# Sharing the weight splits of units 28 to 63 between VectorE and GpSimd in a two-block kernel

## The reference

```python
# first block
h = _rmsnorm(x, norm_g); proj = h @ w_in + b_in                  # 1024 -> 8192
u, v, za, ab, ab_gate, zb, g_a, g_b = split(proj)
y_a = spatial_gating(gelu(u), gelu(v), za)                        # layer norm, 8 masked 128x128 mixes
y_b = conformer_conv(ab * sigmoid(ab_gate), zb)                   # 31-tap depthwise conv, group norm, silu
merged = sigmoid(g_a) * (y_a @ w_pa) + sigmoid(g_b) * (y_b @ w_pb)
x = x + merged @ w_out
x = x + sigmoid(_rmsnorm(x, ple_norm_g) @ w_ple_gate) * (p @ w_ple)
x = _rmsnorm(x, final_g)
# second block
proj = rms_norm(x) @ w_in_2      # qa ka va qb kb vb qi ki wi xc yc gates
y_a = causal attention with a bias table (8 heads)
y_b = attention over the 64 keys with the largest index scores (8 heads)
y_c = rg_lru(conv4(xc)) * gelu(yc)
merged = g0 * (y_a @ w_pa) + g1 * (y_b @ w_pb) + g2 * (y_c @ w_pc)
x = x + merged @ w_o
x = x + relu(rms_norm(x) @ w_up) ** 2 @ w_down
return rms_norm(x)
```

## Time and profile before

| | us |
|---|---|
| median of 3 runs | 820.05 |
| lowest and highest | 819.63, 822.71 |
| the profiled execution | 820.05 |
| its span | 818.2 |

### The profile page before, as it was taken

How to read it: one execution, slowest core, us unless ns; L and a number is a source line. 1 busy time by engine, 2 the same in 40 slices (tenths; PEclk the granted TensorE clock), 3 DMA queues, 4 the chain that set the end, 5 groups by cost and what they waited for, 6 DMA issues and landing times.

```text
span 818.2 us, 14164 instructions
## 1 busy us (share of the span) xinstructions
PE 794.9 (97%) x5914; PEld 751.3 (92%) x5914; DVE 539.8 (66%) x870; ACT 393.7 (48%) x472; POOL 163.4 (20%) x101
## 2 busy tenths in 40 slices
PE   5999999999999998999999999999999999999996
PEld 4998999999989998899999989898999999999995
DVE  4674693999766757766898665555677554545553
ACT  4634354555653457623564435445335644444342
POOL 2898587972000010000003210000000000000000
PEclk8999999999999999989999999999999999999999
DMA  8765454546526586454446544534544655565521
GB/s 251 235 205 157 141 161 140 173 148 209 178 90 205 180 299 191 114 171 155 155 126 196 171 148 133 155 130 146 190 155 155 214 170 183 203 205 189 165 107 52
DMA packets 120625, 138.15 MB, mean 169 GB/s; under 512 B 6704, under 2 KB 111480, under 8 KB 120569
## 3 DMA queue, kind: packets, MB, share of 16 engines
q1 hardware_dynamic: 120089, 135.78, 52.0%
q0 software_dynamic: 480, 1.57, 0.7%
HBM read 133.15 MB, written 4.19 MB: 168 GB/s over the span
## 4 chain that ended last, share of the span: by engine, by line
PE 85%; DVE 9%; ACT 3%; issue 1%; POOL 1%; DMA 1%; SPq 1%; DVEq 0%; ACTq 0%
PE unit L1402 21%; PE unit L1404 20%; PE unit L1403 20%; PE misc L1767 4%; PE misc L1769 4%; PE misc L1770 4%; DVE misc L893 2%; DVE s_wlo L828 2%; ACT s_whi L498 2%; PE misc L1644 1%; PE misc L1665 1%; PE unit L1437 1%; PE unit L1439 1%; PE unit L1441 1%; PE misc L1654 1%
## 5 line engine op out<-in xcount | busy, mean ns | idle before, releaser
L1402 PE MATMUL unit<-s_a_hi,s_whi 128*128 128x256 f32 x816 | 231.8, 284 | 3.9 <-DVE s_wlo L828 3.9
L1403 PE MATMUL unit<-s_a_lo,s_whi 128*128 128x256 f32 x816 | 230.9, 283 | 0.0
L1404 PE MATMUL unit<-s_a_hi,s_wlo 128*128 128x256 f32 x816 | 230.9, 283 | 0.0
L498 ACT ACTIVATE s_whi<-s_raw 128x2048 fp32r<-128x2048 f32 (+2 forms) x94 | 176.6, 1881 | 62.7 <-PE unit L1404 41.6
L828 DVE TENSOR_TENSOR s_wlo<-s_raw,s_whi 128x2048 fp32r<-128x2048 f32 (+1 forms) x69 | 154.9, 2248 | 70.5 <-ACT s_whi L498 70.3
L1402 PE MATMUL unit<-s_b_hi,s_whi 128*128 128x256 f32 x568 | 165.3, 291 | 0.0
L1403 PE MATMUL unit<-s_b_lo,s_whi 128*128 128x256 f32 x568 | 162.3, 286 | 0.0
L1404 PE MATMUL unit<-s_b_hi,s_wlo 128*128 128x256 f32 x568 | 162.3, 286 | 0.0
L1402 PEld LDWEIGHTS unit<-s_a_hi,s_whi 128*128 128x128 f32 x816 | 156.5, 192 | 6.1 <-DVE s_wlo L828 4.7
L1403 PEld LDWEIGHTS unit<-s_a_lo,s_whi 128*128 128x128 f32 x816 | 156.5, 192 | 0.6
L1404 PEld LDWEIGHTS unit<-s_a_hi,s_wlo 128*128 128x128 f32 x816 | 156.5, 192 | 0.0
(11 more groups left out here) (301 smaller groups left out, 1137.4 us busy)
## 6 DMA issues: line engine op xcount, KB each, us to landing
s_raw<-in_w_in SPq DMA_DIRECT2D x62, 1024.0 KB, 5.6
s_raw<-in_w_up SPq DMA_DIRECT2D x16, 1024.0 KB, 5.6
s_raw<-in_w_down SPq DMA_DIRECT2D x16, 1024.0 KB, 5.1
s_raw<-in_w_pa SPq DMA_DIRECT2D x6, 1024.0 KB, 5.5
s_raw<-in_w_pb SPq DMA_DIRECT2D x6, 1024.0 KB, 5.7
s_raw<-in_w_out SPq DMA_DIRECT2D x4, 1024.0 KB, 5.2
s_raw<-in_w_ple_gate SPq DMA_DIRECT2D x4, 1024.0 KB, 7.2
s_raw<-in_w_o SPq DMA_DIRECT2D x4, 1024.0 KB, 5.3
```

The costliest lines, as they stand in the source:

```text
L498: act.activation(ring_view(whi, c), ring_view(raw, c), ACT.Copy).then_inc(Sm["hi_ready"], 1)
L1402: pe.matmul(dst, sh, mh, start=first and k == 0, stop=False)
L1403: pe.matmul(dst, sh, ml, start=False, stop=False)
L1404: ins = pe.matmul(dst, sl, mh, start=False, stop=k == kt - 1)
```

## The change

`SHARED_END` goes from 28 to 64, and POOL's loop runs to that number instead of to the first `gate` unit (46). Of the units 28 to 63 all but 40 (`ple`), 45 (`ple2`) and 52 (`ki`) become shared, 33 in number: DVE subtracts the first 1024 words, POOL the others. PE's `begin` and SP's `load` of the unit three later now wait for both.

```diff
-SHARED_END = 28
+SHARED_END = 64
...
             gp.memset(h_pad[:, :, 0:PAD], 0.0).then_inc(Sm["h_ready"], 1)
-            for c in range(FIRST["gate"] + 1):
+            for c in range(SHARED_END):
                 if c == FIRST["pa"] + 4:
                     gp.wait_ge(Sm["yb_ready"], 4)
```

## The result

The changed kernel took **825.16 us** (median of 19 runs, 822.73 to 829.03), the kernel before 819.83 us (19 runs, 819.08 to 822.71). The ratio is 1.0065, with a 95% interval of 1.0054 to 1.0077: 0.65% slower, 5.3 us. The forecast was 832.3 us with a range of 823.0 to 836.5. The sign and the range held; the size was less than half of the one forecast, and close to rival A (826 us, DVE first). The profiled execution took 826.01 us with a span of 824.1.

A forecast was written before the change was run, and what follows sets the result against it. PE, 97% busy, was taken as the bound, so only longer DVE links it waits for count: 1.2 + 1.2 + 4.1 + 3.5 + 1.7 + 0.6 = 12.3 us on 820.05 gives 832.3 us, range 823 to 836.5.

The forecast's parts named there:

- rival A: Same lock but DVE goes first at shared units: 6.0 us slower, 826 us; chance 0.22.
- What bounds the kernel: PE is busy 97% of the span; only its waits matter, 3.9 us of them for DVE's low halves.
- what a shared unit costs: DVE and POOL halves do not overlap: the unit is complete 3.45 us after rounding, not 2.29, 1.16 us later.
- Rival D: The later, half-sized DVE and POOL instructions overlap, so the gate loop shortens: 816 us; chance 0.05.
- POOL first: At shared units POOL starts ahead and DVE too is held for 3.45 us; the sum assumes this order.
- item 1: Unit 34: DVE's centrings, ACT's squares and PE's variance products come later, +1.2 us (bounds -0.2 to 1.2).
- item 3: Units 42 to 47: late drains, 2.7 us, then the held 4-element chain, 1.4 us; +4.1 us (bounds 0 to 4.1).
- item 2: Unit 41: the merge's last additions and small copy L1027 come later, +1.2 us (bounds 0.5 to 1.2).
- item 5: Units 58 to 60: POOL's half holds twelve L1227, delaying relus before L1710; +1.7 us (bounds 0 to 1.7).
- item 4: Gate loop, units 48 to 50: turn 7.4 us instead of 6.2, whoever is first; +3.5 us (bounds 0 to 3.5).
- item 6: Reciprocals before unit 52 and DVE's row before the first attention head: +0.6 us (0 to 1.2).
- Rival B: Slack hides more: items 3 and 5 and one of 1 and 2 fall away, item 4 halves; 823 us, chance 0.11.

The follow-up runs named there:

- The forced order: The changed kernel, with DVE's half of each shared unit from 28 on (36 excepted) waiting for POOL's half; 841.79 us against 820.91, ratio 1.0246.
- the last experiment's kernel: The changed kernel with the gate stage's splits L1083 of each unit moved behind the next unit's drain; ratio 1.0021 to the kernel before.
- the experiment with these units alone: The kernel before plus units 48, 49 and 50 alone shared; ratio 1.0039, 3.2 us.

## Why the prediction was right, and where it was wrong

**What bounds the kernel** and **what a shared unit costs** held. The pair is serial and complete about 3.5 us after the rounding wherever both engines had been waiting for it (unit 34 and the gate units above). Two readings of the earlier trace rows were off: of the 3.9 us for low halves 1.4 lie at 25.67 us, at unit 1, so the part in reach was 2.5 us; and the 0.2 us at L1512 lie at 173.00 us and not at unit 34:

```profile
173.00 1.24 PE L1512 MATMUL misc<-s_reg_w,s_sel_var 128*4 128x256 f32 x5 [0.23 <-ACT s_reg_w L538]
```

At unit 34 (230.75 us) PE waited for 0.02 us. **Rival D** (overlap) is out.

**The step that failed** was "POOL first", taken from one race at unit 1 with 0.03 us between the two starts. By it the sum held DVE for 3.45 us at every link. In the changed kernel's 20 later units in which both engines had been waiting, DVE starts 0.04 to 0.05 us ahead in every one and is free after 1.23 us. So item 1 (+1.2), the cascade of item 3 (+2.7) and more than half of item 2 were not there. Item 5 (+1.7) failed for a reason of its own: the twelve L1227 were not held, they held POOL.

The forced order shows what hangs on this: 14.0 us of new waits, and 19.5 us in all. The sum had 12.3 for a link 1.16 us longer (here 1.48 us, by the drains L1075 at 326.65 and 334.32 us, 7.67 apart against 6.19; that makes 12.3 x 1.48 / 1.16 = 15.7). So the sum was some 4 us too low for its own order as well: by the arrival times items 1 and 2 came to 4.8 us and not 2.4, item 3 to 5.4 and not 4.1, item 4 to 4.4 and not 3.5, item 5 to 2.4 and not 1.7, item 6 to 2.4 and not 0.6.

Item by item, in the profiles (an item is how much later PE gets there, less what it was late already):

1. Unit 34, +1.2 forecast: 0. The lower bound for DVE first was right in kind, as L900 reads PSUM and passes, but there was no wait of 0.2 us to win. With POOL first PE waited 1.5 us here.
2. Unit 41, +1.2 forecast, 0.5 as the bound for DVE first: +0.4, by L1022 held for 0.7 us. With POOL first the wait grew by 3.3 us, almost three times the item; that several late halves in a row add up is the likely reason.
3. Units 42 to 47, +4.1 forecast: +0.8. The cascade through 42 to 46 (2.7 of it) did not exist, since DVE was free after 1.23 us and drained on time. The 1.4 for the 4-element chain was there as a mechanism, with 0.8 us here and 1.0 us alone. The forecast named the chain's tensor_tensors; here it is a one-input tensor_scalar that is held (in the last experiment's kernel it is the tensor_tensor L1058, for 2.29 us).
4. Gate loop, +3.5 forecast: +3.2 (three turns of 7.25 against 6.19 us); 3.2 us by the experiment with these units alone. This was the item with the same answer for both orders, and it carries most of the result.
5. L1227, +1.7 forecast: 0. Not because the twelve were free of the lock, but because they kept POOL out. With POOL first PE waited 2.2 us at L1710.
6. Two tight places, +0.6 forecast: +0.3, at L1644, and nothing at the reciprocals before unit 52. With POOL first L1644 waited 2.2 us.

The sum of these is 0.4 + 0.8 + 3.2 + 0.3 = 4.7 us, against 5.3 us between the medians. The profiled spans differ by 5.9 us; 1.6 us of that is the lower granted clock from 345 to 400 us, of which I can't say how much belongs to the change. Where the 0.6 us between the sum and the medians come from is not settled either. The stretch at 1.2 GHz near 317 us (granted clock 0.89 from 312 to 327) cost nothing, as PE waited 0.9 us for the next low half behind it in any case.

**Rival A** gave 826 us with 0.5 + 1.4 + 3.5 + 0.8 and -0.2. Each of its terms was measured within 0.6 us; it had 22 in 100, less than half of what the other order had. The evidence for the order was a single start, and with both ends at hand (6.0 and 12.3 us) a forecast between them would have fitted it better. **Rival B** (823 us) had items 3 and 5 nearly right and item 4, of which it took half, wrong.

The Trainium skill, page "SBUF — State Buffer", section "SBUF: two separate sides", says that the pair's lock covers DVE instructions with two SBUF inputs and those in a 2-port mode, and that the one that starts first keeps it for its whole instruction. The trace agrees for scalar_tensor_tensor (3.00 us against 0.87), which was open, and shows the lock for the one-input tensor_scalar L1059 too (2.38 us against 0.17).

## What to carry to other kernels

Where two engines take turns on one resource, splitting a piece of work between them makes the piece as late as the sum of both; it can pay only where the first engine's time is short and what follows on it does not need the same resource, and no run here shows a gain from it. Look at the instruction *behind* the split one on each engine before looking at the split itself: moving the two splits L1083 by one place was worth 3.6 us in the changed kernel, and 1.6 us in the old one, which no sharing from unit 28 on improved. When the sum hangs on who wins a race, work both orders out and put the forecast by how much evidence there is for either.

## What was unexpected of the hardware

- POOL can be starved. Its half of unit 58 needs 2.39 us and took 7.07 us, 7.08 us with units 51 and up alone shared: DVE's twelve L1227 of 0.40 us, each with two SBUF tensors, stood back to back with DVE's own half of unit 58 behind them, and POOL got no turn between them. Where DVE's 4-element instructions are chained by semaphores, with about 0.04 us between them, POOL did get in (310.81 us), and held one for 2.38 us.
- Released by the same rounding, DVE starts 0.04 to 0.05 us ahead of POOL (225.69 and 225.74, 274.58 and 274.62, 320.44 and 320.49 us, 20 cases). In the race near 22 us, which the prediction rested on, POOL is 0.02 to 0.03 us ahead in both kernels; why, I did not find out.
- Three one-element memsets ahead of a subtraction on DVE took only 0.02 us off its lead over POOL (it starts at 221.59 us, POOL at 221.61). But behind the row of L1227 they were enough to let a waiting POOL in (the half of 3.38 us at 397.02 us).
